# First transfers on one queue in the order of need, squares behind the parts of x, and biases written as rows and repeated within memory

## The reference

```
x = first_block(...)    # per layer:
    u = rms_norm(x, norm_mix_g[layer]);  proj = u @ w_in[layer]
    y_a = fourier_mix(a_in); y_b = gqa_branch(...); y_c = mlstm_branch(...); y_d = diff_branch(..., rel_bias, ...)
    merged = sum(sigmoid(gates) * branch);  x = x + merged @ w_out;  x = x + conv_ffn(rms_norm(x), ...)
return second_block(x, ...)   # two layers of windowed attention (rel_bias_2), pooling, latent attention, gated FFN
```

## Time and profile before

| | us |
|---|---|
| median of 3 runs | 3461.98 (3460.44 to 3462.37) |
| the profiled execution | 3460.75 |
| its span in the profile | 3459.4 |

### The profile page before, as it was taken

How to read it: one execution, slowest core, us unless ns; L and a number is a source line. 1 busy time by engine, 2 the same in 40 slices (tenths; PEclk the granted TensorE clock), 3 DMA queues, 4 the chain that set the end, 5 groups by cost and what they waited for, 6 DMA issues and landing times.

```text
span 3459.4 us, 39042 instructions
## 1 busy us (share of the span) xinstructions
PE 3348.3 (97%) x14332; PEld 2555.1 (74%) x14332; DVE 1518.1 (44%) x2800; ACT 1394.1 (40%) x2610; POOL 1406.1 (41%) x1052
## 2 busy tenths in 40 slices
PE   7999999999999989999999999898999999899999
PEld 4667776787888766777688888764688887478887
DVE  4543556444435454456634464447322234732222
ACT  2353335533323345343544333356433235643322
POOL 1223333345555322333344555423255443235544
PEclk8999999999999999999999999999999999999999
DMA  4122221233332211222123332210133322013233
GB/s 152 58 80 64 67 67 62 73 95 113 104 98 93 78 56 64 68 64 68 58 86 120 109 99 95 92 59 28 63 109 99 97 92 74 25 61 110 95 97 101
DMA packets 154882, 284.69 MB, mean 82 GB/s; under 512 B 17984, under 2 KB 20321, under 8 KB 154692
## 3 DMA queue, kind: packets, MB, share of 16 engines
q1 hardware_dynamic: 153204, 279.81, 25.3%
q10 hardware_dynamic: 1488, 2.39, 0.3%
HBM read 276.76 MB, written 5.37 MB: 82 GB/s over the span
## 4 chain that ended last, share of the span: by engine, by line
PE 91%; DVE 4%; ACT 3%; DMA 1%; issue 1%; SPq 0%; POOL 0%; ACTq 0%; DVEq 0%; POOLq 0%
PE bank L544 26%; PE bank L546 25%; PE bank L545 25%; PE bank L602 3%; PE bank L611 2%; PE bank L777 1%; PE bank L791 1%; PE bank L789 1%; PE bank L576 1%; PE bank L911 1%; PE bank L734 1%; PE bank L838 1%; PE bank L659 1%; DMA raw<-in_units 1%; PE bank L622 0%
## 5 line engine op out<-in xcount | busy, mean ns | idle before, releaser
L2056 POOL TENSOR_TENSOR wl<-raw,wh 128x512 fp32r<-128x512 f32 x1012 | 1375.2, 1366 | 2038.2 <-ACT wh L980 2015.2
L544 PE MATMUL bank<-Uh,wh 128*128 128x512 f32 x2720 | 1126.5, 414 | 22.8 <-DVE Ul L1413 19.4
L546 PE MATMUL bank<-Uh,wl 128*128 128x512 f32 x2720 | 1068.3, 393 | 0.0
L545 PE MATMUL bank<-Ul,wh 128*128 128x512 f32 x2720 | 1066.2, 392 | 0.0
L980 ACT ACTIVATE wh<-raw 128x512 fp32r<-128x512 f32 x1012 | 624.7, 626 | 1081.7 <-PE bank L546 1047.4
L544 PEld LDWEIGHTS bank<-Uh,wh 128*128 128x128 f32 x2720 | 515.0, 189 | 187.1 <-issue 62.0
L545 PEld LDWEIGHTS bank<-Ul,wh 128*128 128x128 f32 x2720 | 515.7, 190 | 122.1 <-issue 19.0
L546 PEld LDWEIGHTS bank<-Uh,wl 128*128 128x128 f32 x2720 | 514.3, 189 | 111.5
L1402 DVE TENSOR_TENSOR work<-bank,rs 128x512 f32<-128x512 f32 x308 | 212.7, 691 | 790.9 <-PE bank L546 750.0
L544 PE MATMUL bank<-Hh,wh 128*128 128x512 f32 x1258 | 504.7, 401 | 4.4 <-DVE small L1639 1.9
L546 PE MATMUL bank<-Hh,wl 128*128 128x512 f32 x1258 | 490.3, 390 | 0.0
(11 more groups left out here) (222 smaller groups left out, 2760.6 us busy)
## 6 DMA issues: line engine op xcount, KB each, us to landing
raw<-in_units SPq DMA_DIRECT2D x1012, 256.0 KB, 2.7
xT<-in_xT SPq DMA_DIRECT2D x8, 256.0 KB, 9.9
scratch<-work SPq DMA_DIRECT2D x1, 2048.0 KB, 14.0
out<-xT SPq DMA_DIRECT2D x8, 256.0 KB, 2.9
table<-scratch SPq DMA_DIRECT2D x4, 448.0 KB, 5.3
scratch<-table SPq DMA_DIRECT2D x1, 1152.0 KB, 5.4
work<-in_dft SPq DMA_DIRECT2D x2, 512.0 KB
work<-in_counts SPq DMA_DIRECT2D x2, 512.0 KB, 5.3
```

What stands on the lines that cost most here:

```text
L544: nc.tensor.matmul(out, H, xh, start=k == 0, stop=False)
L545: nc.tensor.matmul(out, H, xl, start=False, stop=False)
L546: mm = nc.tensor.matmul(out, L, xh, start=False, stop=k == x.kt - 1)
L2056: nc.gpsimd.tensor_tensor(g.wl[:, a:a + PK * P], g.raw[:, a:a + PK * P], g.wh[:, a:a + PK * P].bitcast(F32), ALU.subtract).then_inc(g.s_lo, 1)
```

## The change

- `first_loads` on ACT's queue is cut to the vectors of layer 0. Its other transfers go to SP's queue: constants and bias tables (`second_loads`) behind pieces 2 and 3 and ahead of the transforms, the selection matrix, cos and sin, the lambda vectors and the vectors of layer 1 (`third_loads`) behind the transforms. Piece 1 goes behind part 4 of x.
- On ACT all eight `Uh` come first, with pieces 1 and 2 split behind k = 3 and k = 7, then the eight squares, with piece 3 split behind the third. On DVE all eight `Ul` come first, then the sums.
- On PE a0 and a1 come first. The biases take three matmuls of 4, 4 and 6 output rows in place of fourteen of 128, and DVE copies three banks in place of fourteen. The mean of squares follows.
- The biases are written out with one row for each head (`biases`, two transfers), and the other 127 rows of each head are filled by a transfer from memory to memory that reads the one row 127 times (`repeated`, ten transfers: four of 127 x 1024 floats, six of 127 x 384), issued on SP's queue ahead of piece 14, the first of bq0.
- DVE's wait for `scratch1` in `gates_out` goes, and the waits for the tables are for 80 and 112 in place of 16.

```
--- before.py
+++ after.py
@@ -613,29 +613,24 @@
...
+        finish_of(i, "a", 0)
+        finish_of(i, "a", 1)
         if i == 0:
             pe.wait_ge(g.landed["spread1"], 32)
-            for h in range(4):
-                for a in range(2):
-                    b = 2 + (2 * h + a) % 4
-                    take(b, s_dve, "V", "spread1", h, a)
-                    nc.tensor.matmul(bank[b][:, :], g.merged[0:NB, 2 * S + h * P:2 * S + (h + 1) * P],
-                                     g.merged[0:NB, a * S:(a + 1) * S], start=True, stop=True).then_inc(
-                                         s_pe, T("spread1", h, a))
-        finish_of(i, "a", 0)
-        if i == 0:
+            pe.wait_ge(g.landed["spread2"], 32)
+            m = g.merged
+            by_head = m[0:NB, 2 * S:3 * S].rearrange("b (h p) -> b p h", p=P)[:, 0, :]
+            for a in range(2):
+                nc.tensor.matmul(bank[2 + a][0:4, :], by_head, m[0:NB, a * S:(a + 1) * S], start=True, stop=True).then_inc(
+                    s_pe, T("spread", a))
+            by_head = m[0:NB, 4 * S:4 * S + 6 * P].rearrange("b (h p) -> b p h", p=P)[:, 0, :]
+            nc.tensor.matmul(bank[4][0:6, 0:L2], by_head, m[0:NB, 3 * S:3 * S + L2], start=True, stop=True).then_inc(
+                s_pe, T("spread", 2))
+            for a in range(3):
+                take(2 + a, s_dve, "V", "spread", a)
             pe.wait_ge(g.landed["const"], 32)
         norm_mean(i, "mix")
         beat(i, "F", 0)
-        if i == 0:
-            pe.wait_ge(g.landed["spread2"], 32)
-            for h in range(6):
-                b = 2 + h % 4
-                take(b, s_dve, "V", "spread2", h)
-                nc.tensor.matmul(bank[b][:, 0:L2], g.merged[0:NB, 4 * S + h * P:4 * S + (h + 1) * P],
-                                 g.merged[0:NB, 3 * S:3 * S + L2], start=True, stop=True).then_inc(
-                                     s_pe, T("spread2", h))
-        finish_of(i, "a", 1)
         beat(i, "F", 1)
@@ -1154,14 +1149,18 @@
-            split_weights(-RING + 2)
+            split_weights(-RING + 1)
             act.wait_ge(g.landed["vec0"], VEC_LANDED[0])
             for k in range(KD):
                 act.wait_ge(g.s_x[k], 16)
                 nc.scalar.activation(tile(g.Uh, k), tile(g.xT, k), ACT.Copy, scale=g.v1(0, "mix", k)).then_inc(
                     s_act, C("Uh", 0, "mix", k))
+                if k % 4 == 3:
+                    split_weights(-RING + 2 + k // 4)
+            for k in range(KD):
                 model_tile(0, "mix", k, None, w(25 + k % 2))
-                split_weights(-RING + 2 + k // 2)
+                if k == 2:
+                    split_weights(0)
             act.wait_ge(g.landed["const"], 32)
@@ -1506,8 +1505,6 @@
         dve.wait_ge(s_act, at("C", "rs", i, "mix"))
-        if i == 0:
-            dve.wait_ge(g.landed["scratch1"], 16)
@@ -1810,27 +1807,21 @@
         if i == 0:
-            rows = g.work[:, 17 * S:25 * S]
-            for h in range(4):
-                for a in range(2):
-                    b = 2 + (2 * h + a) % 4
-                    dve.wait_ge(s_pe, at("T", "spread1", h, a))
-                    nc.vector.tensor_copy(rows[:, h * L1 + a * S:h * L1 + (a + 1) * S], bank[b][:, :]).then_inc(
-                        s_dve, V("spread1", h, a))
             dve.wait_ge(g.landed["vec0"], VEC_LANDED[0])
             for k in range(KD):
                 dve.wait_ge(g.s_x[k], 16)
-                model_tile(0, "mix", k, g.v1(0, "mix", k), w(25 + k % 2))
+                lower(tile(g.Ul, k), tile(g.xT, k), tile(g.Uh, k), ("C", "Uh", 0, "mix", k), "U", 0, "mix", k,
+                      scale=g.v1(0, "mix", k))
+            for k in range(KD):
+                model_tile(0, "mix", k, None, w(25 + k % 2))
+            for a, rows, cols in ((0, 4, S), (1, 4, S), (2, 6, L2)):
+                dve.wait_ge(s_pe, at("T", "spread", a))
+                nc.vector.tensor_copy(g.table[0:rows, a * S:a * S + cols], bank[2 + a][0:rows, 0:cols]).then_inc(
+                    s_dve, V("spread", a))
         else:
             dve.wait_ge(g.landed[f"vec{i % 2}"], VEC_LANDED[i])
         nc.vector.tensor_scalar(gq, g.v1(i, "q"), HQ ** -0.5, None, ALU.mult).then_inc(s_dve, V())
         beat(i, "F", 0)
-        if i == 0:
-            for h in range(6):
-                b = 2 + h % 4
-                dve.wait_ge(s_pe, at("T", "spread2", h))
-                nc.vector.tensor_copy(g.table[:, h * L2:(h + 1) * L2], bank[b][:, 0:L2]).then_inc(
-                    s_dve, V("spread2", h))
         beat(i, "F", 1)
 
         def features(p):
@@ -2120,23 +2111,35 @@
  
+    def biases(scratch, a, rows, L, name):
+
+        sp.wait_ge(g.s_dve, at("V", "spread", a))
+        nc.sync.dma_start(scratch[:, 0:1, :].rearrange("h p l -> h (p l)"),
+                          g.table[0:rows, (a // 2) * 2 * S:(a // 2) * 2 * S + L]).then_inc(landed[name], 16)
+
+    def repeated(scratch, rows, L, name):
+        sp.wait_ge(landed[name], 16)
+        for h in range(rows):
+            row = bass.AP(tensor=scratch.tensor, offset=h * P * L, ap=[[0, P - 1], [1, L]])
+            nc.sync.dma_start(scratch[h:h + 1, 1:P, :].rearrange("h p l -> (h p) l"), row).then_inc(landed[name], 16)
+
     weights(1)
-    x_tile(0)
-    weights(2)
-    for k in range(1, KD):
+    for k in range(KD):
         x_tile(k)
+        if k == 4:
+            weights(2)
     weights(4)
+    second_loads(g)
     transforms()
-    sp.wait_ge(g.s_dve, at("V", "spread1", 3, 1))
-    nc.sync.dma_start(A["scratch1"].rearrange("h p l -> p h l"),
-                      g.work[:, 17 * S:25 * S].rearrange("p (h l) -> p h l", h=4)).then_inc(landed["scratch1"], 16)
+    third_loads(g)
     weights_before(0, "a", 3)
-    sp.wait_ge(g.s_dve, at("V", "spread2", 5))
-    nc.sync.dma_start(A["scratch2"].rearrange("h p l -> p h l"),
-                      g.table[:, 0:6 * L2].rearrange("p (h l) -> p h l", h=6)).then_inc(landed["scratch2"], 16)
+    biases(A["scratch1"], 1, 4, L1, "scratch1")
+    biases(A["scratch2"], 2, 6, L2, "scratch2")
+    weights_before(0, "bq", 0)
+    repeated(A["scratch1"], 4, L1, "scratch1")
+    repeated(A["scratch2"], 6, L2, "scratch2")
     weights_before(0, "cq", 0)
-    sp.wait_ge(landed["scratch1"], 16)
-    sp.wait_ge(landed["scratch2"], 16)
+    sp.wait_ge(landed["scratch1"], 16 * 5)
     for h in range(4):
         nc.sync.dma_start(g.table[:, h * E1:(h + 1) * E1], skewed(A["scratch1"], h, L1, E1)).then_inc(
             landed["table1"], 16)
@@ -2148,7 +2151,7 @@
             vectors_of(g, nc.sync, i + 1)
             extras_of(g, nc.sync, i + 1)
         if i == 0:
-            sp.wait_ge(landed["scratch2"], 16)
+            sp.wait_ge(landed["scratch2"], 16 * 7)
             transforms()
             extras_of(g, nc.sync, 1)
         else:
@@ -2185,29 +2188,33 @@
     queue.dma_start(to[:, 0:n], src[:, a:a + n]).then_inc(g.landed["extra"], 16)
 
 
-def first_loads(g):
-
-    nc, A, landed = g.nc, g.A, g.landed
-    m, (sel, n), (eps, _) = g.merged, CONST["select"], CONST["eps"]
-    vectors_of(g, nc.scalar, 0)
-    nc.scalar.dma_start(m[0:NB, 0:L1], A["onehot1"]).then_inc(landed["spread1"], 16)
-    nc.scalar.dma_start(m[0:NB, 2 * S:3 * S], A["rb1"]).then_inc(landed["spread1"], 16)
-    nc.scalar.dma_start(g.const[:, 0:sel], A["const"][:, 0:sel]).then_inc(landed["const"], 16)
-    nc.scalar.dma_start(g.const[:, eps - n:NCONST - n], A["const"][:, eps:NCONST]).then_inc(landed["const"], 16)
-    nc.scalar.dma_start(m[0:NB, 3 * S:3 * S + L2], A["onehot2"]).then_inc(landed["spread2"], 16)
-    nc.scalar.dma_start(m[0:NB, 4 * S:4 * S + 6 * P], A["rb2"]).then_inc(landed["spread2"], 16)
+def second_loads(g):
+
+    nc, A, landed, m = g.nc, g.A, g.landed, g.merged
+    sel, (eps, _), n = CONST["select"][0], CONST["eps"], CONST["select"][1]
+    nc.sync.dma_start(g.const[:, 0:sel], A["const"][:, 0:sel]).then_inc(landed["const"], 16)
+    nc.sync.dma_start(g.const[:, eps - n:NCONST - n], A["const"][:, eps:NCONST]).then_inc(landed["const"], 16)
+    nc.sync.dma_start(m[0:NB, 0:L1], A["onehot1"]).then_inc(landed["spread1"], 16)
+    nc.sync.dma_start(m[0:NB, 2 * S:3 * S], A["rb1"]).then_inc(landed["spread1"], 16)
+    nc.sync.dma_start(m[0:NB, 3 * S:3 * S + L2], A["onehot2"]).then_inc(landed["spread2"], 16)
+    nc.sync.dma_start(m[0:NB, 4 * S:4 * S + 6 * P], A["rb2"]).then_inc(landed["spread2"], 16)
+
+
+def third_loads(g):
+    nc, A, landed, m = g.nc, g.A, g.landed, g.merged
+    (sel, n), (eps, _) = CONST["select"], CONST["eps"]
     for rows in (slice(0, HQ), slice(HQ, P)):
-        nc.scalar.dma_start(m[rows, 6 * S:6 * S + n], A["const"][0:HQ, sel:sel + n]).then_inc(landed["select"], 16)
-    nc.scalar.dma_start(g.const[:, sel:eps - n], A["const"][:, sel + n:eps]).then_inc(landed["select"], 16)
-    extras_of(g, nc.scalar, 0)
-    vectors_of(g, nc.scalar, 1)
+        nc.sync.dma_start(m[rows, 6 * S:6 * S + n], A["const"][0:HQ, sel:sel + n]).then_inc(landed["select"], 16)
```

(5 more changed lines are left out.)

## The result

| | us |
|---|---|
| the changed kernel, median of 4 runs | 3546.71 (3546.65 to 3549.74) |
| the kernel before, median of 4 runs | 3462.18 (3460.44 to 3462.54) |
| ratio | 1.0245, 95% interval 1.0232 to 1.0257 |
| the changed kernel's profiled execution, its span | 3546.65, 3545.3 |

The change made the kernel 84.5 us slower. The prediction was 3540, range 3505 to 3590.

A forecast was written before the change was run, and what follows sets the result against it. PE, busy 97% of the span, was taken to lose or win time only where it waits or runs slowly. 3460.75 + 78.4 (bq0 later) = 3539.2; with the median 1.2 higher, 3540, range 3505 to 3590.

The forecast's parts named there:

- The main step: Ten repeats ahead of piece 14: all on one engine at 25 GB/s, 130 us, PE standing about 100 us at bq0.
- Rival 1: Repeats: spread over all engines, 12 us, the start's gain stands; 3440, or 3450 with a poorer start; chance 0.09.
- step 4: Behind bq0: nothing else late; the slow clock after the stand takes some 2.5 us, put at nothing.
- Rival 2: Repeats: one engine, slower within memory, 260 us and 3670, or a third slower, 3583; chance 0.07 for over 25 us more.
- rival 3: Start: gains nothing as SP's single queue brings piece 4 late; repeats begin at 72, time 3562; chance 0.07.
- (1): Start up to a2: first step at 37.5 against 62.88, 25.4 us won, of which 3 given back.
- (2): Start of the repeats, behind piece 13 on SP: at 50, against piece 13's issue at 72.25 before.
- (3): Start of bq0: piece 14 lands at 184.3, bq0 comes at 186.4 against 108.00 before, 78.4 us late.
- step 5: PE's wait of 5.08 us at 123: may shrink as DVE has time for the gates, put at nothing.

The follow-up runs named there:

- The spread kernel: The changed kernel with each repeat of 127 rows cut into one of 112 rows and one of 15; 3451.36 us, ratio 0.9964.
- the experiment on the order: The changed kernel with a1 put back behind the mean of squares in layer 1 alone; 3535.44 us, ratio 1.0212 against the kernel before.

## Why the prediction was right

**The main step held.** Nothing in the trace before showed a transfer within memory; the price was taken from the nearest row, a load of as many rows on the same queue. One engine, 125 us in place of 130, and PE's stand of 94.9 in place of about 100. The rule of the Trainium skill (page "DMA: Bandwidth & Descriptors", section "Why a DMA increments its semaphore by 16 and not by 1") holds for memory to memory in these runs: 127 rows gave a share of 0.06, 122 rows 0.13, 112 rows 0.9. All three shares fit powers of two as well, as said above. The way to the wait was the one on record too: of the 129.3 us from the first repeat to the landing of piece 14, SP was held in the repeats' issues for 112.77, and the rest went to the issue of the piece and its wait behind the engine. Rival 1 (spread over all engines, 3440, or 3450 with a poorer start) did not occur. The spread kernel took 3451, 11 us above its main figure though the start was better than forecast; it has PE's stand of 5.1 us at layer 1 too (step 4), which rival 1 did not price either. Rival 2 fell with 25 to 26 GB/s, rival 3 with a2 at 35.72.

**Steps, one by one.**

(1) Start: a2 was forecast at 37.5 and came at 35.72. The working had a0 and a1 at the slow level of the clock until 25.5; in fact matmuls are 0.23 apart from 10.4 us on. The bias matmuls of 512 columns took 0.86 us each at that level, half of the 1.75 that they took with 128 output rows at the slow one, so that fewer rows don't shorten them held. PE is through with the mean at 24.0, and then waits 5.95 us for the transforms and 3.26 for piece 4. So of the two limits that the prediction put level, the transfers were the one that bound: piece 4 at 33.6 where 35 was said.

(2) Repeats from 47.96 where 50 was said.

(3) bq0 at 178.77 where 186.4 was said: 5 us from the pace, 2 from the start, the rest from piece 14's split. That term was too high by 7.6 us.

(4) Behind bq0 the prediction had nothing, and there are 15.1 us. For the same matmuls PE is busy for 11.3 us longer there and idle for 3.8 longer. The idle time is about the 5.1 us of standing at layer 1, less what step 5 wins. The busy time is the clock: by the granted clock, read in windows of 5 us, PE spends some 77 us behind bq0 at the slow level, and 55 in the kernel before; at half the pace, the 22 us more cost 11. Of these, 2.3 lie right behind the stand, where products are 0.43 apart until 184; the prediction had priced them at 2.5 and put them at nothing. About 2 follow the stand at layer 1. The order of a1 and the mean thus costs 7 in all, of standing and clock. I read the change as one of layer 0 and missed that these lines run for both layers; the experiment on the order confirms it. The rest, near 7, is in spells at the slow level that both kernels have and that last longer in the changed one: behind the wait at bq1 products are 0.43 apart for 1.4 us before (to 127.3) and for 3.6 us after (198.0 to 201.6). What makes them longer is not settled.

(5) PE's wait at bq1 was taken as it is, and shrank from 5.08 to 4.17.

So the time was hit to 0.2% by luck: (3) was 7.6 us too high and (4) 15.1 too low. What was forecast with a mechanism, the delay at bq0, measured 70.8 us where 78.4 was said.

## What to carry to other kernels

Count the rows of every transfer along its outermost dimension. In these runs 127 rows, a number with no divisor, put it all on one engine at some 26 GB/s, and cutting off 15 rows to leave 112 cost one more issue. Compare the length of that work with what is ready ahead on the queue (30 us here): the weights that PE waited for stood behind it. Whether another queue would have spared them was not tried. And when a line moves in a loop over layers, price the move in each of them; the first layer's cover is not the second's.

## What the runs showed of the hardware

How long SP is held by an issue depends on what is ahead in the queue. With no repeat just ahead of it, each of the ten repeats took 0.57 to 0.65 us to issue in the kernel that spreads them among the pieces. In the row of ten the first took 0.66 and the second 7.47; the third to fifth took 19.69 each, though the fifth is one of 190.5 KB, and the last four 7.73. I read this as an issue being held until a transfer ahead of it is through; that of piece 14, behind them all, took 7.70. The load of the transforms took 5.01 us to issue, with two other loads just ahead.

The clock: in the kernel before, PE ran 33-row matmuls for 14.03 us from 7.32 on the earlier trace rows, and after a gap of 1.5 us the products behind them were still 0.43 apart (1.2 GHz). In the changed kernel 128-row products from 6.82 on were 0.23 apart (2.4 GHz) from 10.4. The column of the granted clock reads 1.00 in both stretches; at the start of an execution only the distance of the matmuls tells it.
